# Stick-breaking attention taken head by head through eight banks, with the latents' norm moved ahead of it and the gates' sigmoid moved beside the next product

## The chip, the core and the metric

The kernel runs on one core of a Trainium2 chip. The core's engines work in parallel, each on its own stream of instructions: TensorE (PE, matmuls; PEld is its weight load), VectorE (DVE), ScalarE (ACT), GpSimd (POOL) and SyncE (SP). They wait for each other through semaphores. The metric is the device time of one execution in microseconds (us), median of several runs.

## The reference, cut to what matters

The program is a transformer layer followed by a second one, each on 256 tokens of width 2048, in fp32. The change lies in the first layer, in this part of it:

```
proj = h @ w_in                      # 2048 -> 8256 columns, split into:
c_q, c_kv (512 each), k_pe (64), q_sb, k_sb, v_sb (1024 each), gl_a, gl_b (2048 each)
# stick-breaking attention, 8 heads of 128
z = (q_sb @ k_sb.T) * 128 ** -0.5;   mask = key < query
log_beta = log_sigmoid(z)
log_one_minus = where(mask, log_sigmoid(-z), 0)
tail = reverse_cumsum(log_one_minus) - log_one_minus
a = where(mask, exp(log_beta + tail), 0);   y_b = a @ v_sb
# latents
q = rms(c_q) @ w_uq;   kv = rms(c_kv) @ w_ukv
merged = sigmoid(gl_a) * (y_a @ w_proj_mla) + sigmoid(gl_b) * (y_b @ w_proj_sb)
```

Beside all this runs `ada = silu(c) @ w_ada`, a product of one row with a matrix of 2048 x 12288.

## The kernel before

**Products with weights.** A `Gemm` takes its weights in chunks of 128 partitions x 1024 elements (512 KB). Per chunk: SP loads `raw` (four buffers, queue of SP); ACT makes the rounded half `w_hi` (L402, four buffers); DVE makes the rest `w_lo = raw - w_hi` (L431, two buffers), which also frees the `raw` buffer; PE does eight matmuls with `w_hi` (L462, the activations too are split into a high and a low half) and four with `w_lo` (L467). A full-speed chunk takes PE 2.72 us. `g_in` is `h @ w_in`; its last 64 columns are done by `Narrow` (L258 to L283). `g_psb` is the product with `w_proj_sb`, 4 units of 4 chunks; `evac_gate_b` (L1021) multiplies its result by the gate out of PSUM. `g_uq` and `g_ukv` follow. The functions in `g.beside` run between the chunks of one engine's stream.

**`ada`** is spread in slots beside other work. One slot (`ada.multiply`) is two DVE instructions (L336 at a block's start, L338 later) on one of four buffers of `w_ada`, 512 KB here, which POOL reloads when a slot has used it. Eight slots are a block, closed by one sum (L343); PE sums the block over partitions (`ada.sum`, L354) and DVE takes it (`ada.take`, L366). The table `stations` says how many slots stand at each place; the station `(None, 0, 0)` is the attention.

**The attention between `g_in` and `g_psb`.** Every engine's stream is written out by hand, in this order:

- PE transposes q and k (L586, 32 matmuls, ring `ps_turn` of three PSUM banks), DVE copies them out (L701). PE computes the masked scores of eight heads (L724 to L727) in a ring of the four banks `ps_gemm`; DVE copies each to `zs` (L754, 128 x 384).
- By halves of four heads (128 x 1536): DVE makes abs(z) (L758), ACT makes exp(-abs z) (L782) and ln(1 + that) (L786), DVE makes `mz` = max(z,0) + that (L764) and writes min(z,0) - that back to `zs` (L766). Four `ada` slots stand between L758 and L764.
- PE makes the tails of each head from `mz` (L735 to L737); DVE subtracts them from `zs` (L770); ACT takes exp (L789); PE multiplies with v (L745, L746); ACT and DVE split the result into `yt_hi` (L792) and `yt_lo` (L774).
- DVE does four more `ada` slots; ACT does the latents' squares and root (L662, L666) behind `yt_hi`; DVE inverts and scales the latents (L676, L966); PE transposes them (L498, two latents of two units each, eight matmuls a latent); ACT and DVE split them (L558, L538). The second latent's transposes wait until the first is split. Then `g_psb` starts.

ACT also does the sigmoid of both gates (L798, two instructions of 4096 elements) before the attention's own work. A change of ACT's function set costs an `ACT_TABLE_LOAD`.

Of the kernel before, what the change touches and what calls it, by code (L numbers as in the profile page):

```python
# [15 lines left out]
P = 128  # L16
# [127 lines left out]
def program(nc, A, out):  # L144
# [560 lines left out]
    z_filled, z_copied, z_abs, z_soft = sem("z_filled"), sem("z_copied"), sem("z_abs"), sem("z_soft")  # L705
    m_ready, lb_ready = sem("m_ready"), sem("lb_ready")
    tail_filled, arg_ready, a_ready = sem("tail_filled"), sem("arg_ready"), sem("a_ready")
# [253 lines left out]
    def lat_vector(dve):  # L961
# [5 lines left out]
        for turn in turn_lat:  # L967
            turn.vector(dve)
# [1685 lines left out]
```

## Time and profile before

| what | value |
| --- | --- |
| median of 3 runs | 2732.0 us (2729.41 to 2737.89) |
| the profiled execution | 2730.92 us; span from its first to its last instruction 2729.0 us |
| mean granted TensorE clock | 0.984 of full speed |
| busy share of the span | PE 95%, DVE 62%, ACT 43%, POOL 5% |
| `w_lo` (L431), mean of one | 1.22 us |
| the chain that ended last | PE 91%, DVE 5%, issue 1%, DMA 1%, ACT 1% |

The profile page divides the span in 40 slices of 68 us and gives tenths of busy time. The PE row reads 9 almost throughout, with a 6 in the slice of the attention (409 to 477 us), where DMA reads 2 and 98 GB/s. In a timeline, a row is one or several like instructions: start, time they cover, engine, line, tiles, and in brackets the idle time before the first with what ended it. A granted clock of 1.00 is 2.4 GHz and 0.50 is 1.2 GHz.

### The profile page before, as it was taken

To read this page: it belongs to the slowest core of one execution; us is meant where nothing else is said; L and a number is where in the kernel's file an instruction comes from. 1 tells how busy PE (TensorE), PEld (TensorE's weight loads), DVE (VectorE), ACT (ScalarE), POOL (GpSimd) and SP (SyncE) were. 2 spreads that over 40 slices of the span, in tenths; PEclk is the share of its full clock that TensorE was granted. 3 is DMA by queue.
4 is the path that set the end of the run, shared out by engine and by line. 5 is a ranking of instruction groups with operands and counts; after the bars stand their busy time and mean duration, and the time that the engine had idled before them with its cause. 6 is when DMAs were issued, how large, how long until landed. Compare 5 with 4: busy or idle time off the path is not lost.

```text
span 2729.0 us, 33054 instructions
## 1 busy us (share of the span) xinstructions
PE 2592.2 (95%) x12109; PEld 2142.2 (78%) x12109; DVE 1691.5 (62%) x2227; ACT 1180.0 (43%) x1506; POOL 149.2 (5%) x211
## 2 busy tenths in 40 slices
PE   3999996959989999999999999999999999999998
PEld 3878885747878888888888888878878888888886
DVE  6888987788867764545445565457654545454444
ACT  2543434334454444444334544534454444444443
POOL 1211110111101100000000000000000000000000
PEclk9999998989999999999999999999999999999999
DMA  8988892846958866666655656531366666665554
GB/s 303 332 282 273 298 313 98 293 144 223 322 159 281 278 206 192 185 192 200 192 193 190 190 162 183 179 117 47 120 189 186 191 187 190 189 188 185 194 194 158
DMA packets 269003, 559.41 MB, mean 205 GB/s; under 512 B 22784, under 2 KB 24528, under 8 KB 268240
## 3 DMA queue, kind: packets, MB, share of 16 engines
q1 hardware_dynamic: 235216, 453.57, 53.2%
q0 software_dynamic: 26752, 96.48, 10.7%
q10 hardware_dynamic: 6912, 7.73, 0.8%
q8 instruction: 76, 1.25, 0.2%
q14 instruction: 47, 0.39, 0.0%
HBM read 555.60 MB, written 2.11 MB: 204 GB/s over the span
## 4 chain that ended last, share of the span: by engine, by line
PE 91%; DVE 5%; issue 1%; DMA 1%; ACT 1%; SPq 0%; DVEq 0%; ACTq 0%
PE ps L462 55%; PE ps L467 28%; DMA ada_raw<-in_w_ada 1%; PE ps L498 1%; DVE acc L338 1%; PE ps L2311 1%; PE ps L1398 1%; PE ps L354 1%; PE ps L2167 1%; DVE acc_odd L338 1%; DVE w_lo L431 0%; PE ps L2340 0%; PE ps L276 0%; PE ps L2322 0%; ACT w_hi L402 0%
## 5 line engine op out<-in xcount | busy, mean ns | idle before, releaser
L431 DVE TENSOR_TENSOR w_lo<-raw,w_hi 128x1024 fp32r<-128x1024 f32 x846 | 1033.6, 1223 | 848.4 <-PE ps L467 773.1
L402 ACT ACTIVATE w_hi<-raw 128x1024 fp32r<-128x1024 f32 x846 | 893.5, 1062 | 1165.6 <-PE ps L467 439.7
L462 PE MATMUL ps<-w_hi,xt_hi 128*128 128x512 f32 x2496 | 987.8, 396 | 14.8 <-ACT w_hi L402 10.6
L462 PE MATMUL ps<-w_hi,xt_lo 128*128 128x512 f32 x2496 | 976.0, 391 | 0.0
L467 PE MATMUL ps<-w_lo,xt_hi 128*128 128x512 f32 x2496 | 669.3, 390 | 0.3 <-DVE w_lo L431 0.3
L462 PEld LDWEIGHTS ps<-w_hi,xt_hi 128*128 128x128 f32 x2496 | 470.8, 189 | 115.7 <-issue 11.2
L467 PEld LDWEIGHTS ps<-w_lo,xt_hi 128*128 128x128 f32 x2496 | 469.5, 188 | 100.2 <-DVE w_lo L431 1.4
L462 PEld LDWEIGHTS ps<-w_hi,xt_lo 128*128 128x128 f32 x2496 | 471.2, 189 | 94.7
L462 PE MATMUL ps<-w_hi,ht_hi 128*128 128x512 f32 x704 | 274.7, 390 | 0.0
L462 PE MATMUL ps<-w_hi,ht_lo 128*128 128x512 f32 x704 | 274.0, 389 | 0.0
L467 PE MATMUL ps<-w_lo,ht_hi 128*128 128x512 f32 x704 | 188.2, 389 | 0.0
L314 POOL DMA_DIRECT2D ada_raw<-in_w_ada x192 | 138.8, 723 | 825.8 <-DVE acc_odd L338 576.8
L467 PEld LDWEIGHTS ps<-w_lo,ht_hi 128*128 128x128 f32 x704 | 132.1, 188 | 27.5
L462 PEld LDWEIGHTS ps<-w_hi,ht_lo 128*128 128x128 f32 x704 | 132.2, 188 | 27.3
L462 PEld LDWEIGHTS ps<-w_hi,ht_hi 128*128 128x128 f32 x704 | 132.2, 188 | 27.2
L338 DVE SCALAR_TENSOR_TENSOR acc<-ada_raw,ccol,acc 128x512 f32<-128x512 f32 (+1 forms) x182 | 128.1, 704 | 10.2 <-DMA ada_raw<-in_w_ada 10.1
L338 DVE SCALAR_TENSOR_TENSOR acc_odd<-ada_raw,ccol,acc_odd 128x512 f32<-128x512 f32 (+1 forms) x182 | 128.0, 703 | 0.0
L462 PE MATMUL ps<-w_hi,yt_hi 128*128 128x512 f32 x128 | 51.8, 405 | 3.7 <-ACT w_hi L402 3.7
L462 PE MATMUL ps<-w_hi,yt_lo 128*128 128x512 f32 x128 | 50.9, 398 | 0.0
L2507 POOL DMA_DIRECT2D w1k<-in_cmp_w_k x4 | 3.0, 752 | 734.2 <-PE ps L467 734.2
L958 DVE TENSOR_TENSOR proj<-ps,proj 128x512 f32<-128x512 f32 x64 | 40.9, 681 | 2.5 <-PE ps L467 2.5
L2383 ACT ACTIVATE pb<-ps,nst 128x128 f32<-128x128 f32 x64 | 26.3, 416 | 36.8 <-DVE nst L2359 36.8
(359 smaller groups left out, 1582.4 us busy)
## 6 DMA issues: line engine op xcount, KB each, us to landing
raw<-in_w_in SPq DMA_DIRECT2D x208, 512.0 KB, 4.6
raw<-in_w_ffn_in SPq DMA_DIRECT2D x176, 512.0 KB, 3.8
ada_raw<-in_w_ada POOLq DMA_DIRECT2D x128, 512.0 KB, 5.6
raw<-in_w_ffn_out SPq DMA_DIRECT2D x88, 512.0 KB, 4.6
raw<-in_w_gate SPq DMA_DIRECT2D x88, 512.0 KB, 3.7
raw<-in_w_up SPq DMA_DIRECT2D x88, 512.0 KB, 4.4
raw<-in_w_down SPq DMA_DIRECT2D x88, 512.0 KB, 4.3
raw<-in_w_out SPq DMA_DIRECT2D x64, 512.0 KB, 4.4
```

Source lines behind the costliest of these rows:

```text
L314: sp.dma_start(self.tile(v), wview("w_ada")[:, ADA_K * s:ADA_K * (s + 1), col:col + width]).then_inc((ada_first if v < 2 * self.per else a ...
L338: ins = dve.scalar_tensor_tensor(part, rows[:, k, :], weight, part, ALU.mult, ALU.add)
L354: mm = pe.matmul(ps_ada[:, at_i:at_i + 1], acc[:, b % 2, i * P:(i + 1) * P], ones[:, 0:1], start=True, stop=True)
L402: act.activation(w_hi[:, w % HI, :, :], raw[:, w % RAW, :, :], ACT.Copy).then_inc(hi_ready, 1)
L431: dve.tensor_tensor(w_lo[:, w % LO, :, :], raw[:, w % RAW, :, :], w_hi[:, w % HI, :, :].bitcast(F32), ALU.subtract).then_inc(raw_used, 1)
L462: pe.matmul(bank[t][:, :], g.lhs(part, g.k0 + 2 * s + k, t), w_hi[:, w % HI, k, :], start=(s == 0 and k == 0 and part == 0), stop=False)
L467: mm = pe.matmul(bank[t][:, :], g.lhs(0, g.k0 + 2 * s + k, t), w_lo[:, w % LO, k, :], start=False, stop=(s == g.S - 1 and k == 1))
L498: mm = pe.transpose(ps_turn[n % 3][:, k * SEQ + t * P:k * SEQ + (t + 1) * P], self.src(2 * v + k, t), ident)
L958: last = nc.vector.tensor_tensor(p, ps_gemm[2 * (c % 2) + t][:, :], p, ALU.add)
L1398: mm = pe.transpose(ps_turn[v][:, k * SEQ + t * P:k * SEQ + (t + 1) * P], hbuf[:, t, (2 * v + k) * P:(2 * v + k + 1) * P], ident)
L2167: mm = pe.matmul(ps_ada[0:60, 0:256], fl[i][:, u, :, :].rearrange("p h i -> p (h i)"), w1[i][:, u, :], start=(u == 0), stop=(u == 15))
L2311: pe.matmul(bank[:, lo:up], qrT[:, 4 * a + m, t * P:(t + 1) * P], ksw[br][:, a, b, 0:(t + 1) * P], start=True, stop=False)
```

## The change

1. **By head.** abs, exp and ln are done per head, in place in `mz` (named `soft(h)`); abs moves from DVE to ACT. The write-back of min(z,0) - ln(...) is gone: PE's matrices become minus (strictly after or equal) and minus ones (`neg_upto`, `neg_ones`, made by two DVE instructions), so that z plus the bank is the argument of exp. Scores, and then tails, have one bank per head out of all eight; the products with v use banks 0 to 3.
2. **`ada`.** Six slots instead of eight stand in the attention: three behind the scores, one each behind the arguments of heads 0, 2 and 4. The other two stand in units 0 and 1 of `g_psb`, which then have one beside every chunk. The take of the last block of `g_in` stands before the attention.
3. **Latents.** Squares and root stand on ACT ahead of `Narrow`'s copy; inverse and scaling stand on DVE ahead of the attention. The transposes stay behind it.
4. **Gates.** The sigmoid is four ACT instructions of 2048 elements, one behind each of the first four `w_hi` of `g_psb`.

```diff
 def sb_tensor(pe):
+        pe.wait_ge(ada_taken, ada.sums)
         for h in range(H):
-            pe.wait_ge(turn_scaled, turn_sb.at + 2 * (h // 2) + 2)
-            if h - 3 > 0:
-                pe.wait_ge(z_copied, h - 3)
-            b = ps_gemm[h % 4]
+            pe.wait_ge(turn_scaled, turn_sb.at + (2 * (h // 2) + 2 if h < 5 else 8))
+            b = ps[h]
...
         for h in range(H):
-            pe.wait_ge(m_ready, h // 4 + 1)
-            pe.matmul(b[:, 0:SEQ], after, mz[h // 4][:, h % 4, 0:SEQ], start=True, stop=False)
+            pe.wait_ge(m_ready, h + 1)
+            pe.matmul(b[:, 0:SEQ], neg_upto[:, :], soft(h)[:, 0:SEQ], start=True, stop=False)
...
 def sb_vector(dve):
-        ada.multiply(dve, 4)
+        ada.multiply(dve, 3)
         for h in range(H):
+            dve.wait_ge(z_log, h + 1)
+            dve.scalar_tensor_tensor(soft(h), zs[:, h, :], 0.0, soft(h), ALU.max, ALU.add).then_inc(m_ready, 1)
+        for h in range(H):
             dve.wait_ge(tail_filled, h + 1)
-            dve.tensor_tensor(zs[:, h, :], zs[:, h, :], ps_gemm[h % 4][:, 0:BL], ALU.subtract).then_inc(arg_ready, 1)
+            dve.tensor_tensor(zs[:, h, :], zs[:, h, :], ps[h][:, 0:BL], ALU.add).then_inc(arg_ready, 1)
+            if h in SB_SLOTS:
+                ada.multiply(dve, SB_SLOTS[h])
...
+    def gates_piece(act, i):
+        if i == 0:
+            act.wait_ge(evac_done, g_in2.c + 1)
+        c0, c1 = ((GB0, NIN), (GA0, GB0))[i // 2]
+        act.activation(proj[:, i % 2, c0:c1], proj[:, i % 2, c0:c1], ACT.Sigmoid).then_inc(gates_ready, 1)
+    SB_SLOTS = {0: 1, 2: 1, 4: 1}
...
-    stations += [(None, 0, 0, 8)]
-    stations += [(g_psb, u, s, 1 if s < 3 else 0) for u in range(4) for s in range(4)]
+    stations += [(None, 0, 0, 6)]
+    stations += [(g_psb, u, s, 1 if s < 3 or u < 2 else 0) for u in range(4) for s in range(4)]
...
 def _(act):
+            rms_lat.scalar(act)
             g_in2.copied(act)
             g_in2.scalar(act, lambda t: proj[:, t, 8192:NIN])
-            gates_scalar(act)
             sb_scalar(act)
-            rms_lat.scalar(act)
...
 def _(dve):
+            lat_vector(dve)
+            ada.take(dve, len(ada_takes[None, 0, 0]))
             sb_vector(dve)
-            ada.multiply(dve, 4)
-            lat_vector(dve)
-            dve.wait_ge(gates_ready, 2)
+            lat_turns_vector(dve)
```

ACT's stream from `Narrow`'s copies to the attention's last exp, before (`ez` is the buffer of four heads each):

```order
L263 ACTIVATE proj<-ps 128x64 x2
L798 ACT_TABLE_LOAD
L798 ACTIVATE proj<-proj 128x4096 x2
L782 ACT_TABLE_LOAD
L782 ACTIVATE ez<-ez 128x1536 x2
L786 ACT_TABLE_LOAD
L786 ACTIVATE ez<-ez,const 128x1536 x2
L789 ACT_TABLE_LOAD
L789 ACTIVATE zs<-zs 128x384 x8
```

The same place now, for the first two of the eight heads and then the end:

```order
L263 ACTIVATE proj<-ps 128x64 x2
L775 ACTIVATE mz_99<-zs 128x384
L777 ACT_TABLE_LOAD
L777 ACTIVATE mz_99<-mz_99 128x384
L775 ACTIVATE mz_99<-zs 128x384
L777 ACTIVATE mz_99<-mz_99 128x384
...
L780 ACT_TABLE_LOAD
L780 ACTIVATE mz_99<-mz_99,const 128x384 x4
L780 ACTIVATE mz_100<-mz_100,const 128x384 x4
L783 ACT_TABLE_LOAD
L783 ACTIVATE zs<-zs 128x384 x8
```

The two long sigmoids are gone from here; abs (L775) and exp (L777) alternate with a single table load, and ln (L780) follows for all heads.

DVE's stream from the last `yt_lo` to the first `w_lo` of `g_psb`, before (`acc`, `acc_odd` are slots of `ada`):

```order
L774 TENSOR_TENSOR yt_lo<-ps,yt_hi 128x512 x4
L338 SCALAR_TENSOR_TENSOR acc<-ada_raw,ccol,acc 128x512
L338 SCALAR_TENSOR_TENSOR acc_odd<-ada_raw,ccol,acc_odd 128x512
...
L343 TENSOR_TENSOR acc<-acc,acc_odd 128x512
L676 RECIPROCAL stat<-stat 128x4
L966 TENSOR_SCALAR proj<-proj,stat 128x512 x4
L538 SCALAR_TENSOR_TENSOR lat_lo<-ps,cols,lat_hi 128x256 x8
L431 TENSOR_TENSOR w_lo<-raw,w_hi 128x1024
```

And now:

```order
L767 TENSOR_TENSOR yt_lo<-ps,yt_hi 128x512 x4
L538 SCALAR_TENSOR_TENSOR lat_lo<-ps,cols,lat_hi 128x256 x8
L431 TENSOR_TENSOR w_lo<-raw,w_hi 128x1024
```

The four slots, the block's sum, the inverse and the scaling no longer stand between `yt_lo` and the latents' split.

ACT's stream at the start of `g_psb` now (before, the `w_hi` rows follow each other):

```order
L558 ACTIVATE lat_hi<-ps,cols 128x256 x8
L402 ACTIVATE w_hi<-raw 128x1024
L793 ACT_TABLE_LOAD
L793 ACTIVATE proj<-proj 128x2048
L402 ACTIVATE w_hi<-raw 128x1024
L793 ACTIVATE proj<-proj 128x2048
```

Each of the first four conversions is followed by a piece of the sigmoid.

## Rows read from the trace of the kernel before

**Rows 1.** Two stretches, all engines; busy us, count, granted clock, DMA share, GB/s.

```profile
434.64:445.06 10.42, 0.00 (x0) 0.00 (x0) 10.35 (x13) 7.89 (x6) 2.89 (x4) 0.64 0.36 108
...
461.88:469.76 7.88, 0.00 (x1) 0.01 (x1) 7.75 (x15) 3.30 (x8) 2.89 (x4) 0.68 0.58 174
```

**Rows 2.** DVE in order of time: start us, us, line, out<-in, [idle before <-releaser].

```profile
428.68 0.54 DVE L754 COPY zs<-ps 128x384 f32<-128x384 f32 x1
...
434.68 0.56 DVE L754 COPY zs<-ps 128x384 f32<-128x384 f32 x1 [0.32 <-PE ps L727]
...
435.15 3.42 DVE L758 SCALAR_TENSOR_TENSOR ez<-zs 128x1536 f32<-128x1536 f32 x2
...
439.28 0.74 DVE L338 SCALAR_TENSOR_TENSOR acc<-ada_raw,ccol,acc 128x512 f32<-128x512 f32 x1
...
443.25 1.75 DVE L764 SCALAR_TENSOR_TENSOR mz<-zs,ez 128x1536 f32<-128x1536 f32 x1
...
468.03 1.67 DVE L966 TENSOR_SCALAR proj<-proj,stat 128x512 f32<-128x512 f32 x4
```

**Rows 3.** ACT in order of time, same columns.

```profile
421.61 0.38 ACT L258 ACTIVATE w_in_rest_turned<-ps 64x256 f32<-64x256 f32 x1 [12.80 <-PE ps L276]
...
424.06 7.13 ACT L798 ACTIVATE proj<-proj 128x4096 f32<-128x4096 f32 x2
...
440.11 1.28 ACT L786 ACT_TABLE_LOAD   x1
...
441.40 3.04 ACT L786 ACTIVATE ez<-ez,const 128x1536 f32<-128x1536 f32 x2
...
444.46 1.28 ACT L789 ACT_TABLE_LOAD   x1
...
450.76 1.45 ACT L789 ACTIVATE zs<-zs 128x384 f32<-128x384 f32 x3 [5.02 <-DVE zs L770]
```

**Rows 4.** PE in order of time, same columns.

```profile
423.22 4.47 PE L586 MATMUL ps<-const,proj 128*128 128x128 f32 x32
...
445.06 1.22 PE L735 MATMUL ps<-mz,const 128*128 128x256 f32 x2 [10.42 <-DVE mz L764]
...
455.12 0.60 PE L745 MATMUL ps<-zs,proj 128*128 128x256 f32 x2
...
460.14 0.38 PE L746 MATMUL ps<-zs,proj 128*128 128x128 f32 x2
...
469.76 1.97 PE L498 MATMUL ps<-const,proj 128*128 128x128 f32 x8 [9.23 <-DVE proj L966]
...
473.57 1.97 PE L498 MATMUL ps<-const,proj 128*128 128x128 f32 x8 [1.84 <-DVE lat_lo L538]
```

**Rows 5.** The chain of waits: start us, us, what.

```profile
474.72 0.84 ACT lat_hi L558 x2
...
476.41 0.95 ACT w_hi L402
...
477.50 3.75 PE ps L462 x8
...
481.25 1.25 PE ps L467 x4
...
486.18 1.81 PE ps L462 x8
```

**Rows 6.** Two stretches of 2 us in which the granted clock falls.

```profile
436.00:438.00 2.00, 0.00 (x0) 0.00 (x0) 2.00 (x2) 1.07 (x1) 0.00 (x0) 0.87 0.00 0
...
464.00:466.00 2.00, 0.00 (x0) 0.00 (x0) 2.00 (x4) 1.20 (x2) 0.95 (x2) 0.69 0.52 100
```

**Rows 7.** ACT's conversion of chunk 7 of the product with w_proj_sb.

```profile
492.98 1.06 ACT L402 ACTIVATE w_hi<-raw 128x1024 fp32r<-128x1024 f32 x1 [2.66 <-DMA raw<-in_w_proj_sb]
```

**Rows 8.** The chain at the same chunk.

```profile
499.93 1.81 PE ps L462 x8
```

**Rows 9.** Ten us with one w_ada slot beside every chunk.

```profile
170.00:180.00 10.00, 10.00 (x49) 8.38 (x48) 8.97 (x14) 3.86 (x4) 2.60 (x4) 1.00 0.97 330
```

More of the change, by code:

```diff
@@ L704, in program @@
                      for d, c, s in ((qsb, Q0, sb_scale), (ksb, K0, 1.0))])
-    z_filled, z_copied, z_abs, z_soft = sem("z_filled"), sem("z_copied"), sem("z_abs"), sem("z_soft")
-    m_ready, lb_ready = sem("m_ready"), sem("lb_ready")
-    tail_filled, arg_ready, a_ready = sem("tail_filled"), sem("arg_ready"), sem("a_ready")
+    z_filled, z_copied, z_abs, z_exp, z_log = (sem(f"z_{n}") for n in ("filled", "copied", "abs", "exp", "log"))
+    m_ready, neg_ready, arg_ready = sem("m_ready"), sem("neg_ready"), sem("arg_ready")
+    tail_filled, a_ready = sem("tail_filled"), sem("a_ready")
     yb_filled, yb_hi, yb_lo = sem("yb_filled"), sem("yb_hi"), sem("yb_lo")
@@ L778, in sb_scalar @@
     def sb_scalar(act):
-        for f in range(2):
-            ef = ez[:, 4 * f:4 * f + 4, :].rearrange("p a b -> p (a b)")
-            act.wait_ge(z_abs, f + 1)
-            act.activation(ef, ef, ACT.Exp, scale=-1.0).then_inc(z_abs2, 1)
-        for f in range(2):
-            ef = ez[:, 4 * f:4 * f + 4, :].rearrange("p a b -> p (a b)")
-            act.wait_ge(z_abs2, f + 1)
-            act.activation(ef, ef, ACT.Ln, bias=ones[:, 0:1]).then_inc(z_soft, 1)
+        act.wait_ge(turn_scaled, turn_sb.end)
+        for h in range(H):
+            act.wait_ge(z_copied, h + 1)
+            act.activation(soft(h), zs[:, h, :], ACT.Abs).then_inc(z_abs, 1)
+            act.wait_ge(z_abs, h + 1)
+            act.activation(soft(h), soft(h), ACT.Exp, scale=-1.0).then_inc(z_exp, 1)
+        for h in range(H):
+            act.wait_ge(z_exp, h + 1)
+            act.activation(soft(h), soft(h), ACT.Ln, bias=ones[:, 0:1]).then_inc(z_log, 1)
         for h in range(H):
@@ L1018, in evac_gate_b @@
         col = Count(GB0 + CW * u, 2 * CW, j).value
+        if u == 0 and j is None:
+            nc.vector.wait_ge(gates_ready, 4)
         for t in range(T):
@@ L1480, in program @@
             ada_sums.setdefault(later[1] if g else later[0], []).append(done)
-            ada_takes.setdefault(later[2] if g else later[1], []).append(done)
+            taken = later[1] if g and later[1][0] is None else later[2] if g else later[1]
+            ada_takes.setdefault(taken, []).append(done)
             done += 1
```

56 lines of the change are left out of this document (20 added, 36 removed).

## The prediction

> **What bounds the kernel now.** I read the page first: PE is busy 95% of the span and carries 91% of the chain, so time can only be won where PE waits. The slices show one such place inside the change's reach, the attention at 421 to 477 us. I then took the windows of that place, the timelines of DVE, ACT and PE, and the chain. Three things are to be seen.
>
> First, between scores and tails PE does nothing for 10.42 us while DVE works 10.35 of them [rows 1]. DVE copies the last score from 434.68, spends 3.42 us on abs, then four slots of w_ada (a slot is two instructions of 0.74 us that overlap a little, 1.33), and begins `mz` at 443.25 [rows 2]; the first tail starts at 445.06 [rows 4]. Second, the tails run 445.06 to 455.12 and the products with v until 460.52 (460.14 + 0.38), back to back. Third, PE is idle again for 9.23 us, until the latents are scaled [rows 4]: DVE is busy 7.75 of 7.88 us with slots, inverse and scaling [rows 1]. The latents' two rounds follow, 469.76 and 473.57 [rows 4], then `g_psb` at 477.50 [rows 5]. So the stretch is a chain of DVE and ACT work, hardly PE's.
>
> **The change part by part.**
>
> *The beginning.* The latents' squares and root go into ACT's idle 12.80 us before 421.61 [rows 3]; about 4 us of work is covered entirely. Inverse and scaling (1.67 us, [rows 2]) fall where DVE waits for the first transposes, so they are free too. New ahead of DVE's first copy are a take and the two instructions that make the matrices. They follow PE's sum, which ends when the transposes begin at 423.22 [rows 4]; the first unit of transposes takes 4.47 / 8 = 0.56 us, which covers most of them. I charge +0.15 us; the nearest rows bound it between 0 and one more 0.74 us instruction.
>
> *Scores to first tail.* DVE's copies start 0.86 us apart ((434.68 - 428.68) / 7) [rows 2]. ACT's chain starts when the first is out, 428.68 + 0.54 + 0.15 = 429.4. Abs and exp of 384 elements have the shape of the exps in [rows 3]: three in 1.45 us, so 0.52 for one and 0.465 for each overlapped. Abs, table load 1.28, exp: 429.4 + 0.55 + 1.28 + 0.52 = 431.8. Seven more pairs, each waiting on its own abs (0.52 + 0.04 + 0.47 = 1.03): 439.0. Load 1.28: 440.3. The two ln of 1536 take 3.04 together [rows 3]; for 384 I estimate 0.6 for one and 0.51 apart. First ln out at 440.9, last at 444.4. DVE has done its three slots by 439 (435.4 + about 3.5), so it is ACT that ends last here. One `mz` of 384 is like the copy, 0.56 us: the first tail starts at 441.5 against 445.06, **-3.55 us**. The bounds are zero gain (ACT's many small instructions eat it) and -6 us (ACT as fast as DVE's copies come).
>
> The ln and exp loads here stand in the chain, where before they stood beside DVE's work. The row of the load shows 1.28 us and the next ACT instruction begins at 441.40, 0.01 us after its end [rows 3]. The Trainium skill (ScalarE: Activation LUTs, What ACT_TABLE_LOAD costs) adds a drain of 1.38 us to each load's 1.283, 2.66 in all; by that the two loads ahead of the first tail would cost 2.8 us more and the time would be 2720.3. The trace disagrees with the drain, so I leave it out.
>
> *Tails and products.* As before, PE has idled over 5 us by 441.5. The clock fell 2.9 us after the first stop (0.87 over 436 to 438 puts the fall at 437.5) and 4.2 us after the second (0.69 over 464 to 466 puts it at 464.8) [rows 6]. So the tails begin at the lower level, 1.2 GHz, as they did, and take the same 10.06 us: 451.6. DVE must keep up: the arguments start behind the last `mz`, 445.0, and take 8 x 0.5 + 3 slots x 1.33 = 8.0 us, so the last is out at about 453 and its exp at 453.5. The product of the last head is due at 451.6 + 7 x 0.675 = 456.3, so PE remains the bound, with 2.8 us to spare. Products end at 451.6 + 5.40 = 457.0. Moving slots in between the arguments costs nothing while that spare lasts.
>
> *Products to latents.* The wait of 9.24 us (460.52 to 469.76) goes: scaled latents are ready, their banks free. **-9.24 us.** What is late next is ACT, which must do the last `yt_hi` before the first `lat_hi`: 0.69 us behind the products' end, where the cold transposes took 469.76 to 470.91, 1.15 us (the first split of the second round starts at 474.72, 1.15 behind 473.57) [rows 4, 5]. That is -0.46. The second round's transposes take 0.6 at 2.4 GHz instead of 1.15, -0.55. The ends from the same rows are 0 and -1.0 for both together, **-1.0 us**. From the second split to PE's start everything is as before (474.72 to 477.50, 2.78). Sum: 477.50 - 3.55 - 9.24 - 1.0 = 463.7, a gain of 13.8.
>
> *The first chunks of g_psb.* Chunk 0 took 3.75 + 1.25 = 5.0 us at 1.2 GHz where a full-speed chunk takes 1.81 + 0.91 = 2.72 [rows 5]. Two things now meet. PE's pauses before it become two of about 2.3 us instead of one of 9.2 and two of 1.8, and both observed falls needed 2.9 and 4.2 us of idleness, so the clock may stay up. But ACT now puts a load and 1.85 us of sigmoid behind each conversion (7.13 / 4 = 1.8 plus start-up) [rows 3]: conversion 1 is out 4.2 us after conversion 0, later ones 2.85 apart. With the high clock PE then waits 1.4 us for chunk 1 and 0.13 for each of the next two, and reaches chunk 4 at 4 x 2.72 + 1.4 + 0.26 = 12.5 us from its start, against 5.0 + 3 x 2.72 = 13.2 at the low clock (a sum over partitions of some 0.8 us comes on top of either). With the low clock ACT is hidden and nothing changes. I take the middle, **-0.4 us**.
>
> [...]
>
> *The two slots moved into g_psb.* On DVE a chunk with a slot costs 1.22 (the page's mean for `w_lo`) + 1.33 = 2.55 us against PE's 2.72, and `w_lo` may be 3 us late before PE notices; hidden. On DMA, units 0 and 1 ask for 1.049 MB per 2.72 us, 385 GB/s. The stretch with one smaller slot (512 + 384 KB a chunk, 337 GB/s asked) ran at 330 GB/s with PE busy 10.00 of 10 us [rows 9]. At 330 the extra 1.05 MB put the loads 3.2 us behind. ACT's conversion of chunk 7 ends at 494.04 and PE takes it at 499.93: 5.9 us of cover [rows 7, 8]. So 0, and 3.2 us if that cover is gone; the value taken is 0.
>
> **Sum.** -3.55 - 9.24 - 1.0 - 0.4 = -14.2 (the +0.15 is inside the first term). The span goes from 2729.0 to 2714.8; with the 1.9 us outside it the profiled execution, 2730.92, becomes 2716.7. The median before, 2732.0, stands 1.1 above its profiled execution; the forecast is 2732.0 - 14.2, rounded to 2717.5 us.
>
> **The rivals.**
>
> *Cover lost in g_psb.* Conversions behind four sigmoids, and loads at 385 GB/s, make PE wait. For it: ACT's cadence, 2.85, is above PE's 2.72, and ACT waits for DMA at chunk 7 already (2.66 us) [rows 7]. Against it: 5.9 us of cover. Price 2 us (sigmoids with a high clock) to 6 us (3.2 more from DMA): 2720 to 2724, centre 2721.5.
>
> *The attention itself gains nothing.* ACT has 24 small instructions, 16 of them in a dependent chain; if each dependent pair costs 0.5 us more than estimated, the first tail starts at 445 again and only the latents' part remains: 2732.0 - 10.6 = 2721.4. For it: ACT is what ends last there. Against it: waits between engines in these timelines cost some 0.04 us.
>
> *The clock stays up.* If it does not fall before 441.5, the tails save up to 3.0 us (eight heads at 0.88 instead of 10.06), and chunk 0 its 0.4: 2714. Against it: the falls at 2.9 and 4.2 us of idleness.
>
> *Slower.* `g_psb` starved by its loads. Units 0 and 1 need 8.4 MB; at a rate R they take 8.4 / R instead of 21.8 us. Above 230 GB/s the loss, with the cover counted, stays below the gain; at 200 GB/s it is 42 - 21.8 - 5.9 = 14.3 us and the time 2732; at 170 GB/s it is 21.7 us and the time 2739. It decides from about 200 GB/s down. Against it: 330 GB/s over ten us with the same two queues [rows 9].
>
> **How the numbers follow.** Forecast 66%, own range 2714 to 2720.5; cover lost 17%; no gain in the attention 8%; clock up 6%; slower 3%. About 0.3%, 8.2 us, is what a measurement of this kernel can tell from no change: the line lies at 2723.8. All of the forecast and the clock case, and most of the next two, lie below it: faster 0.89. Same 0.08 is the upper end of the two middle cases, slower 0.03. The range 2712.5 to 2723.5 takes in both ends of the forecast and nearly all of the middle cases.
>
> **What would show it.** Right: the first tail at 441 to 442 with ACT's ln before it; one 10 us run of tails; the latents' transposes at once behind the products; `g_psb` at 463 to 464.5; PE gapless in `g_psb` but for at most 2 us before chunk 1; the rest of the trace shifted by 14 us. Wrong: table loads between abs and exp; a wait of an argument or an exp that PE feels; PE waiting for `w_hi` with a DMA behind it in chunks 5 to 10; or a later stage that takes the gain back.

## The result, and the profile after

| | before | after |
| --- | --- | --- |
| median | 2733.68 us (2729.41 to 2737.89, 4 runs) | 2718.28 us (2714.57 to 2720.21, 4 runs) |
| the profiled execution | 2730.92 us, span 2729.0 us | 2719.46 us, span 2716.9 us |

The ratio is 0.9942, with an interval of 0.9922 to 0.9962: 15.4 us off the median. The two profiled executions show only 12.1 of them in their spans: the one before is 2.8 us faster than its median, the one after, the slowest but one of its four, 1.2 us slower.

PE in order of time in the kernel after, same columns as [rows 4]. Line numbers moved by a few; L742 and L743 are now the products with v.

```profile
440.14 1.19 PE L735 MATMUL ps<-mz,neg_upto 128*128 128x256 f32 x2 [6.49 <-DVE mz L759]
...
448.70 0.60 PE L742 MATMUL ps<-zs,proj 128*128 128x256 f32 x2
...
453.73 0.38 PE L743 MATMUL ps<-zs,proj 128*128 128x128 f32 x2
453.95 1.04 PE L498 MATMUL ps<-const,proj 128*128 128x128 f32 x8
457.22 1.09 PE L498 MATMUL ps<-const,proj 128*128 128x128 f32 x8 [2.24 <-DVE lat_lo L538]
460.57 0.77 PE L462 MATMUL ps<-w_hi,yt_hi 128*128 128x512 f32 x1 [2.26 <-DVE lat_lo L538]
...
464.83 0.39 PE L462 MATMUL ps<-w_hi,yt_hi 128*128 128x512 f32 x1
```

The tails start 19.51 us behind `Narrow`'s copy (420.63 below; 445.06 - 421.61 = 23.45 before), the latents' transposes stand right behind the last product, and where PE waited 9.23 us there is nothing. What is left are two short pauses of 2.24 and 2.26 us. ACT, answering to [rows 3]:

```profile
420.63 0.38 ACT L258 ACTIVATE w_in_rest_turned<-ps 64x256 f32<-64x256 f32 x1 [11.10 <-PE ps L276]
...
428.34 0.52 ACT L775 ACTIVATE mz<-zs 128x384 f32<-128x384 f32 x1 [6.57 <-DVE zs L754]
...
437.49 1.28 ACT L780 ACT_TABLE_LOAD   x1
438.79 4.16 ACT L780 ACTIVATE mz<-mz,const 128x384 f32<-128x384 f32 x8
442.96 1.28 ACT L783 ACT_TABLE_LOAD   x1
...
454.15 0.60 ACT L786 ACTIVATE yt_hi<-ps 128x512 fp32r<-128x512 f32 x1 [0.71 <-PE ps L743]
454.64 1.56 ACT L558 ACTIVATE lat_hi<-ps,cols 128x256 fp32r<-128x256 f32 x4
...
459.35 1.07 ACT L402 ACTIVATE w_hi<-raw 128x1024 fp32r<-128x1024 f32 x1
...
463.55 1.05 ACT L402 ACTIVATE w_hi<-raw 128x1024 fp32r<-128x1024 f32 x1
```

and DVE, answering to [rows 2]:

```profile
433.69 0.56 DVE L754 COPY zs<-ps 128x384 f32<-128x384 f32 x1 [0.32 <-PE ps L730]
...
439.43 4.10 DVE L759 SCALAR_TENSOR_TENSOR mz<-zs,mz 128x384 f32<-128x384 f32 x8 [1.75 <-ACT mz L780]
...
449.75 1.47 DVE L762 TENSOR_TENSOR zs<-zs,ps 128x384 f32<-128x384 f32 x3
...
455.51 1.66 DVE L538 SCALAR_TENSOR_TENSOR lat_lo<-ps,cols,lat_hi 128x256 fp32r<-128x256 f32 x4
...
460.46 1.23 DVE L431 TENSOR_TENSOR w_lo<-raw,w_hi 128x1024 fp32r<-128x1024 f32 x1
```

DVE has done its three slots by 437.7 and waits for ACT's first ln [1.75 <-ACT mz L780]: ACT sets the first tail. Two windows, columns as [rows 1], the wait for the tails and ten us inside `g_psb` with a slot beside every chunk:

```profile
433.66:440.14 6.48, 0.00 (x1) 0.03 (x1) 4.70 (x9) 6.33 (x12) 2.17 (x3) 0.71 0.47 134
480.00:490.00 10.00, 10.00 (x45) 8.26 (x44) 9.96 (x15) 4.25 (x4) 2.68 (x4) 1.00 1.01 373
```

In the second PE is busy 10.00 of 10 us while the DMA engines are full and move 373 GB/s.

By pieces, from the copy (421.61, 420.63) on:

| piece | before | after | change | forecast |
| --- | --- | --- | --- | --- |
| copy to first tail | 23.45 | 19.51 | -3.94 | -3.55 |
| tails (first tail to first product) | 10.06 | 8.56 | -1.50 | 0 |
| products with v | 5.40 | 5.41 | 0 | 0 |
| wait for the latents | 9.24 | -0.16 | -9.40 | -9.24 |
| the latents' two rounds | 7.74 | 6.62 | -1.12 | -1.0 |
| sum | 55.89 | 39.94 | -15.95 | -13.8 |
| `g_psb`, chunk 0 to chunk 4 (PE) | 13.96 | 13.27 | -0.69 | -0.4 |

Counted from the copy, the changed kernel is 16 us ahead at `g_psb` and 16.5 at `g_ukv`. From there to `g_pmla`, the product behind MLA attention, it loses 7 us in this execution, in stages that the change doesn't touch: 1.6 in `g_ukv` and 5.3 in MLA attention. PE at the same place of MLA attention in the profiled execution (L1135 are its scores):

```profile
578.04 3.67 PE L586 MATMUL ps<-const,proj 128*128 128x128 f32 x16 [24.58 <-DVE pe_out L1093]
...
590.07 0.74 PE L1135 MATMUL ps<-kT,proj 128*128 128x128 f32 x2
...
591.55 1.17 PE L1135 MATMUL ps<-kT,proj 128*128 128x256 f32 x2
```

and in another execution of the same kernel (experiment `e1_again`):

```profile
589.75 0.44 PE L1135 MATMUL ps<-kT,proj 128*128 128x128 f32 x2
...
590.60 0.65 PE L1135 MATMUL ps<-kT,proj 128*128 128x256 f32 x2
```

The scores take 0.74 and 1.17 us in the one and 0.44 and 0.65 in the other. The windows say why:

```profile
590.00:595.00 5.00, 5.00 (x16) 3.02 (x15) 2.95 (x9) 0.93 (x5) 0.72 (x1) 0.50 0.15 23
```
```profile
590.00:595.00 5.00, 5.00 (x27) 3.03 (x25) 4.87 (x14) 1.83 (x8) 0.72 (x1) 1.00 0.22 48
```

A granted clock of 0.50 against 1.00: the clock, back at 583 after a pause of 24.6 us, fell a second time at 590, 2 us after a pause of 1.14 us had ended (587.88) and with PE working, in one execution and not in the other. `g_ukv` shows the same on a smaller scale. Behind a pause of 1.4 us its first chunk starts at the high clock in both, and in the one execution the clock falls within it:

```profile
530.00:532.00 2.00, 2.00 (x6) 1.54 (x5) 1.85 (x3) 0.11 (x1) 0.35 (x1) 0.52 0.90 295
```
```profile
532.00:534.00 2.00, 2.00 (x10) 1.65 (x10) 2.00 (x4) 0.00 (x0) 0.26 (x1) 1.00 0.84 256
```

The first row is the profiled execution, the second `e1_again` at the same place.

### The profile page after: what moved, and what is told of

It reads as the page before. It is cut to its first block, busy times and chain, and to the rows that moved or that the text cites. A ratio compares the mean times of both kernels' runs of the same rounds, so it can differ in the third digit from the quotient of the medians.

```text
span 2716.9 us, 33069 instructions
## 1 busy us (share of the span) xinstructions
PE 2592.0 (95%) x12109; PEld 2140.9 (79%) x12109; DVE 1684.6 (62%) x2231; ACT 1183.6 (44%) x1527; POOL 149.2 (5%) x211
## 4 chain that ended last, share of the span: by engine, by line
PE 91%; DVE 4%; DMA 2%; ACT 1%; issue 1%; SPq 0%; DVEq 0%; ACTq 0%
PE ps L462 55%; PE ps L467 28%; DMA ada_raw<-in_w_ada 1%; PE ps L1398 1%; PE ps L498 1%; PE ps L354 1%; PE ps L2314 1%; PE ps L2170 1%; DVE acc L338 1%; PE ps L2343 0%; DVE w_lo L431 0%; PE ps L276 0%; DMA raw<-in_w_out 0%; PE ps L1137 0%; DVE acc_odd L338 0%
## 5 line engine op out<-in xcount | busy, mean ns | idle before, releaser
L462 PE MATMUL ps<-w_hi,xt_hi 128*128 128x512 f32 x2496 | 987.0, 395 | 15.1 <-ACT w_hi L402 10.8
```

The lines of the kernel that those rows point to most:

```text
L462: pe.matmul(bank[t][:, :], g.lhs(part, g.k0 + 2 * s + k, t), w_hi[:, w % HI, k, :], start=(s == 0 and k == 0 and part == 0), stop=False)
```

## The experiments

Every kernel was timed beside the kernel before on its own chip. In the tables "stretch" runs from `Narrow`'s copy on ACT to the first `w_lo` of `g_psb`, "tails" is the part of it from the first tail to the first product with v, and "MLA" runs from the first `w_lo` of `g_ukv` to the first of `g_pmla`; all are differences of starts in the profiled execution. All profiled executions, in us:

| kernel | copy at | stretch | tails in it | to `g_ukv` | MLA | rest | span |
| --- | --- | --- | --- | --- | --- | --- | --- |
| before | 421.6 | 55.8 | 10.1 | 67.3 | 87.9 | 2096.3 | 2729.0 |
| after | 420.6 | 39.8 | 8.6 | 66.9 | 94.9 | 2094.7 | 2716.9 |
| e1_again | 420.1 | 41.2 | 10.0 | 67.5 | 88.0 | 2094.9 | 2711.7 |
| e12_again | 421.6 | 39.9 | 8.7 | 66.9 | 94.9 | 2094.9 | 2718.2 |
| e2_norm_alone | 421.8 | 51.2 | 9.4 | 67.3 | 87.9 | 2094.8 | 2723.0 |
| e3_norm_slots | 421.3 | 50.4 | 10.8 | 66.7 | 94.9 | 2094.9 | 2728.1 |
| e4_head_alone | 419.9 | 52.8 | 9.1 | 66.9 | 95.0 | 2097.8 | 2732.4 |
| e5_gates_back | 423.5 | 42.5 | 8.7 | 68.2 | 93.2 | 2097.9 | 2725.4 |
| e6_preload | 418.7 | 39.6 | 9.0 | 66.8 | 94.9 | 2094.7 | 2714.6 |
| e7_lat_ring | 421.8 | 38.3 | 8.6 | 67.0 | 94.7 | 2096.9 | 2718.7 |
| e8_warm | 421.8 | 39.6 | 7.1 | 66.8 | 94.8 | 2094.6 | 2717.7 |
| e9_all | 421.6 | 37.4 | 9.3 | 67.0 | 89.4 | 2098.2 | 2713.6 |
| e10_mla_warm | 424.6 | 41.3 | 10.0 | 67.5 | 95.7 | 2094.6 | 2723.7 |
| e11_all_mla | 420.0 | 37.1 | 8.8 | 67.0 | 87.3 | 2096.2 | 2707.6 |

Copy, stretch, "to `g_ukv`", MLA and rest add up to the span. A stretch repeats within 1.5 us (39.8, 39.9, 41.2, and 41.3 in `e10_mla_warm`, whose edit lies behind it), and all of that is in the tails: without them the four are 31.26 or 31.27 us, and the kernel before is 45.77. The MLA column jumps by 7. It has two parts that come separately: `g_ukv` takes 1.6 us more in seven of the 14 profiles, MLA attention 5.3 to 7.7 more in nine of them, `e3_norm_slots` with the old phases among these. Copy and rest move by up to 5.9 and 3.6 us without any edit there. So a single span or a median of six says less of an edit than its stretch does.

**e1_again and e12_again: the changed kernel unaltered.**

> The changed kernel once more, unaltered. The stretch from ACT's first copy behind the narrow product to PE's first matmul with w_proj_sb took 55.9 us before and 39.9 us after; nearly all of this should repeat. In the changed kernel's profile TensorE's clock fell a second time inside the later attention (590 to 604 us), and that stage took 5.3 us longer than before. Theory: this second fall belongs to how the pauses happen to lie in one execution, so it may be missing here, and the time ratio stays at 0.994 plus or minus 0.0015. Rival: the change shifts that stage so that the fall comes every time; then it is there again and the low stretch is again about 13 us.

> The changed kernel unaltered, beside the three others: the time 2714 to 2719 us. Its profile falls in one of two groups: MLA attention 87.9 us and a span of 2711 to 2713, or 94.9 us and 2716 to 2719. By the theory the two differ in TensorE's low clock 10 to 20 us into the stage's matmuls and in nothing else.

Measured: 2715.24 us (2712.43 to 2720.29, 6 runs), ratio 0.9940 [0.9921, 0.9959], and on the other chip 2720.17 us (2715.48 to 2725.39, 6 runs), ratio 0.9950 [0.9931, 0.9969]. One profile is without the second fall (MLA 88.0, span 2711.7), one has it (94.9, 2718.2). What the profile of the change seemed to lose in MLA attention (the 5.3 us of the expectation, 7 with `g_ukv`) is no part of the change: one kernel shows both. `e12`'s median lies 1.2 us above what its expectation allowed.

The three stretches of the changed kernel differ in one thing, how soon the granted clock is back at 1.00 after the first tail: 3.0 us in the first profile, 3.2 in e12, 5.9 in e1 (and 6.2 in the kernel before). The tails take 8.6, 8.7 and 10.0 us accordingly. The first four chunks of `g_psb`, which also start at the low clock, go the same way: 13.27, 13.34 and 13.95 us on PE, where the kernel before takes 13.96.

**e2_norm_alone: the kernel before with squares, root, inverse and scaling ahead of the attention.**

```diff
+        pe.wait_ge(yb_lo, 4)
         for turn in turn_lat:
...
+            rms_lat.scalar(act)
             g_in2.copied(act)
...
-            rms_lat.scalar(act)
...
+            lat_vector(dve)
             sb_vector(dve)
             ada.multiply(dve, 4)
-            lat_vector(dve)
+            lat_turns_vector(dve)
```

> The kernel before, with only the latents' squares, root, inverse and scaling moved ahead of the attention (the four w_ada slots still stand on DVE between yt_lo and the latents' split; PE waits for yt_lo ahead of the latents' transposes, which their banks need). Theory: of the 9.2 us of idle PE only the norm's 1.9 us and the transposes' start go, because DVE's slots (6.0 us) stand in the same queue: the stretch is 52 us (gain 3 to 4.5 us). Rival, that the norm is the whole wait: 46.5 us.

Measured: 2727.6 us (2723.43 to 2733.71, 10 runs), ratio 0.9980 [0.9966, 0.9995]; stretch 51.2, 4.7 less than before, 0.6 of which is the clock in the tails (9.4 for 10.1). DVE and PE behind the attention:

```profile
461.32 0.74 DVE L338 SCALAR_TENSOR_TENSOR acc<-ada_raw,ccol,acc 128x512 f32<-128x512 f32 x1
...
467.34 1.65 DVE L538 SCALAR_TENSOR_TENSOR lat_lo<-ps,cols,lat_hi 128x256 fp32r<-128x256 f32 x4
```
```profile
461.50 1.07 PE L498 MATMUL ps<-const,proj 128*128 128x128 f32 x8 [1.46 <-issue]
469.05 1.97 PE L498 MATMUL ps<-const,proj 128*128 128x128 f32 x8 [6.48 <-DVE lat_lo L538]
```

PE transposes the first latent 1.46 us behind the products (461.50; this edit has it wait for the last `yt_lo`) and then waits 6.48 us: DVE's split of that latent stands behind four slots and the block's sum. The wait of 9.24 us has moved by one round, and 7.9 of it are still there.

**e3_norm_slots: the same, and the four slots one each behind the arguments of heads 0, 2, 4 and 6.**

```diff
                               ALU.subtract).then_inc(arg_ready, 1)
+            if h % 2 == 0:
+                ada.multiply(dve, 1)
...
-            ada.multiply(dve, 4)
```

> As the run with the norm alone, and the four slots behind yt_lo are put behind the arguments of heads 0, 2, 4 and 6. Heads are not taken singly and the gates' sigmoid stays ahead. Theory: the wait between products and latents is gone, the rest is unchanged: the stretch is 46.5 to 47.5 us (8.5 to 9.4 us less than before), at most 0.5 us lost where the last argument comes late. Rival, that taking the heads singly carries the gain: under 3 us.

Measured: 2731.17 us (2726.03 to 2734.81, 10 runs), ratio 0.9987 [0.9971, 1.0002]; stretch 50.4. The time can't be told from the kernel before. Theory and rival both missed the stretch: 5.4 us less, not 8 to 9, nor under 3. Where it went, DVE, ACT and PE at the end of the products:

```profile
459.09 0.55 DVE L770 TENSOR_TENSOR zs<-zs,ps 128x384 f32<-128x384 f32 x1
```
```profile
460.10 1.55 ACT L794 ACTIVATE yt_hi<-ps 128x512 fp32r<-128x512 f32 x3
```
```profile
461.55 0.67 PE L745 MATMUL ps<-zs,proj 128*128 128x256 f32 x2 [1.96 <-DVE yt_lo L776]
```

By phases the arguments start only when DVE has written `zs` back, and four slots behind them put the last argument at 459.09. The last exp waits for it, `yt_hi` of the first heads is queued behind that exp on ACT, `yt_lo` behind `yt_hi`, and PE's products wait 1.96 us for a bank that `yt_lo` frees. PE's last product ends 2.9 us later than before (41.85 against 38.92 behind the copy), 2.2 of it in the products and 0.7 in the tails, most of which are waits for a bank of the old ring of four. That takes back 2.9 of the 7.8 us of waiting behind the products that went (9.24 before, 1.46 now).

**e4_head_alone: by head in eight banks, and norm, slots and sigmoids where they were.**

```diff
-            rms_lat.scalar(act)
             g_in2.copied(act)
             g_in2.scalar(act, lambda t: proj[:, t, 8192:NIN])
+            for i in range(4):
+                gates_piece(act, i)
             sb_scalar(act)
+            rms_lat.scalar(act)
...
-        ada.multiply(dve, 3)
+        ada.multiply(dve, 4)
...
-    SB_SLOTS = {0: 1, 2: 1, 4: 1}
+    SB_SLOTS = {}
...
-            lat_vector(dve)
             ada.take(dve, len(ada_takes[None, 0, 0]))
             sb_vector(dve)
+            ada.multiply(dve, 4)
+            lat_vector(dve)
             lat_turns_vector(dve)
```

> The changed kernel with only its attention by head kept: norm, sigmoid and w_ada slots stand as before (eight slots, four of them behind yt_lo, sigmoid ahead of the attention). Theory: ACT's sigmoid delays the first abs by 1.9 us, so the first tail comes 2 us earlier than before instead of 3.9; the 9.2 us behind the products are back. The stretch is 52.5 to 54 us. Rival, that heads carry the gain: 44 to 46 us.

Measured: 2735.83 us (2730.9 to 2741.87, 10 runs), ratio 1.0008 [0.9993, 1.0023]; stretch 52.8.

```profile
441.32 1.19 PE L735 MATMUL ps<-mz,neg_upto 128*128 128x256 f32 x2 [8.44 <-DVE mz L759]
...
465.01 1.97 PE L498 MATMUL ps<-const,proj 128*128 128x128 f32 x8 [9.24 <-DVE proj L962]
```

The first tail comes 21.46 us behind the copy, 2.0 earlier than before and 2.0 later than in the changed kernel; then the old wait, 9.24 us for DVE's scaling. By head alone gives 3 us of stretch, 2.0 by the first tail and 1.0 because the clock came back sooner in the tails (9.1 us for 10.1), and no time that these runs can tell.

So norm and slots gain 5.4 us of stretch, by head 3.0, the gates 1.3 to 2.7 (next experiment), together 9.7 to 11.1, and the whole change 14.6 to 16.0. Some 4 to 6 us come only from the parts' meeting. Without the tails, in which the clock differs from one execution to the next, the whole is 14.5. By head, DVE has room for slots between the arguments: the first argument starts 3.3 us behind the first tail (443.45, 440.14), in the old phases 5.1 (450.18, 445.06). But the changed kernel also has two slots and the block's sum less there than e3, and no run moves these two alone, so how the 4 to 6 us divide between room and less work isn't shown.

**e5_gates_back: the changed kernel with the four sigmoid pieces ahead of the attention.**

```diff
+            for i in range(4):
+                gates_piece(act, i)
             sb_scalar(act)
...
-        if u == 0:
-            gates_piece(eng, s)
```

> The changed kernel with the four pieces of the gates' sigmoid ahead of the attention's ACT work again. Theory: the load and the pieces take 8.6 us from 421.8 on ACT, 1.9 us past the point where the first abs could begin, and ACT is the bound between scores and tails: the first tail 1.9 us later, the stretch 41.8 us; the first four chunks of the product with w_proj_sb get back 0.9 us of waits, so about 1 us is lost in all. Rival: it was covered before and still is, no change in the stretch, and 0.9 us gained.

Measured: 2724.17 us (2721.19 to 2729.24, 10 runs), ratio 0.9963 [0.9951, 0.9976]; stretch 42.5, 1.3 to 2.7 more than the changed kernel.

```profile
425.99 7.31 ACT L793 ACTIVATE proj<-proj 128x2048 f32<-128x2048 f32 x4
433.20 0.51 ACT L775 ACTIVATE mz<-zs 128x384 f32<-128x384 f32 x1
```

The first abs waits for the sigmoids (433.20 is 9.67 us behind the copy; in the changed kernel 428.34 - 420.63 = 7.71), and the first tail comes at 21.46 instead of 19.51. That is the 2 us by which by head alone fell short. The 0.9 us that the first chunks were expected to give back did not come: chunk 0 to chunk 4 took 14.64 us on PE, with chunk 0 at the low clock throughout (13.27 and 13.95 in the changed kernel). The median is 4.6 us above the next kernel's beside it. The first tail explains 2 of them; the rest stays unexplained, as the two profiled spans differ by 10.8 us, 4.9 of them ahead of the edit and 3.2 in the column of the rest.

**e6_preload: a one-column exp ahead of the first abs, so that the table load leaves the chain.**

```diff
+            act.wait_ge(eps_set, 1)
+            act.activation(stat[:, 31:32], epsc[:, 0:1], ACT.Exp)
             sb_scalar(act)
```

> The changed kernel with one exp of a single column on ACT ahead of the first abs, so that the exp table is loaded while ACT waits. Theory: ACT's chain is the bound between scores and first tail, so the stretch shortens by the load, 1.3 us (39.9 to 38.6). Rival: DVE or the scores are the bound: no change.

Measured: 2719.60 us (2716.39 to 2722.93, 4 runs), ratio 0.9955 [0.9938, 0.9971]; stretch 39.6.

```profile
436.88 1.19 PE L735 MATMUL ps<-mz,neg_upto 128*128 128x256 f32 x2 [5.20 <-DVE mz L759]
```

The first tail comes 18.23 us behind the copy, 1.28 earlier: just the load. But the clock now falls before the latents' second round instead of behind it (that round takes 1.97 us instead of 1.09), the two rounds take 0.56 us more and the tails 0.45, and 0.3 us are left of 1.3.

**e7_lat_ring: the second latent's transposes wait for their own bank only.**

```diff
-            if max(n - 2, self.at) > 0:
-                pe.wait_ge(turn_scaled, max(n - 2, self.at))
+            first = self.at if self.ring is None else self.ring
+            if max(n - 2, first) > 0:
+                pe.wait_ge(turn_scaled, max(n - 2, first))
```

> The changed kernel with the second latent's transposes waiting for two units back in their ring and not for the whole first latent. Theory: the two rounds behind the products (6.6 us) are bound by that wait; ACT and DVE run through, 1.6 us less (39.9 to 38.3), and the clock of the first chunk may change. Rival: ACT's eight splits in a row bound it: under 0.5 us.

Measured: 2718.73 us (2717.08 to 2720.82, 4 runs), ratio 0.9946 [0.9929, 0.9962]; stretch 38.3, as expected.

```profile
455.15 1.48 PE L500 MATMUL ps<-const,proj 128*128 128x128 f32 x12
457.64 0.66 PE L500 MATMUL ps<-const,proj 128*128 128x128 f32 x4 [1.01 <-DVE lat_lo L540]
```

Twelve matmuls go in one run and the pause is 1.01 us instead of 2.24. In the time it is lost among executions. Chunk 0 of `g_psb` now starts at the high clock (0.47 and 0.40 us a matmul) and falls to the low one with its fifth matmul (0.45, then 0.63).

**e8_warm: 88 small matmuls that nothing reads, in PE's wait for the tails.**

```diff
+        pe.wait_ge(z_copied, H)
+        for _ in range(88):
+            pe.matmul(ps[7][:, 0:P], ident16[:, :], maskz, start=True, stop=True)
         pe.wait_ge(neg_ready, 2)
```

> The changed kernel with 88 small bf16 matmuls (masked constants into a bank that is overwritten later) while PE would idle between scores and tails. Theory: the low clock at the tails goes, 8 x 0.875 = 7.0 us instead of 8.56, the stretch 1.5 us shorter; and the clock stays high until the first chunk of the product with w_proj_sb only if its own pauses don't drop it. Rival: DVE's arguments and ACT's exps follow the tails at 1.0 us a head and eat the gain: under 0.5 us.

Measured: 2716.52 us (2715.29 to 2719.5, 4 runs), ratio 0.9938 [0.9921, 0.9955]; stretch 39.6, 0.2 to 1.6 less than the changed kernel.

```profile
435.50 5.09 PE L733 MATMUL ps<-masks,ident 128*128 128x128 bf16 x88 [0.65 <-DVE zs L757]
441.33 0.67 PE L738 MATMUL ps<-mz,neg_upto 128*128 128x256 f32 x2 [0.75 <-DVE mz L762]
...
452.11 0.70 PE L745 MATMUL ps<-zs,proj 128*128 128x256 f32 x2 [0.24 <-ACT zs L786]
...
457.60 1.97 PE L498 MATMUL ps<-const,proj 128*128 128x128 f32 x8 [2.39 <-DVE lat_lo L538]
```

The clock stays up: the first tail's matmuls take 0.67 us instead of 1.19. But PE now reaches a product before its exp (0.24), the products take 5.9 us instead of 5.4 and end 1.0 us earlier than in the first profile of the changed kernel (2.4 earlier than in e1's), and the second round of the latents is at the low clock (1.97). By the end of the products the tails' low clock costs 1.0 to 2.4 us, as the clock's return falls, since DVE and ACT come next.

**e9_all: the edits of e6 and e7 together, abs of heads 5 to 7 on DVE, and one slot moved from behind the scores to behind the argument of head 6.** The diff shows the last two.

```diff
+            if h > 4:
+                dve.wait_ge(z_copied, h + 1)
+                dve.scalar_tensor_tensor(soft(h), zs[:, h, :], -1.0, zs[:, h, :], ALU.mult, ALU.max).then_inc(z_abs, 1)
-        ada.multiply(dve, 3)
+        ada.multiply(dve, 2)
...
-    SB_SLOTS = {0: 1, 2: 1, 4: 1}
+    SB_SLOTS = {0: 1, 2: 1, 4: 1, 6: 1}
```

> The changed kernel with four edits at once: the exp functions are loaded before the first abs; the abs of heads 5 to 7 is on VectorE; the second latent's transposes wait only for their bank; two slots of w_ada behind the scores and one each behind the arguments of heads 0, 2, 4 and 6. Theory (ScalarE's chain sets the first tail, the latents' ring costs 1.5 us): the first tail starts 17.0 to 17.5 us behind Narrow's copy, where the changed kernel has 19.5; g_psb starts 1.5 us earlier again from the ring; the stretch from that copy to g_psb's first w_lo is 36 to 37.5 us (39.8 and 41.2 in the two profiles of the changed kernel) and the time 2 to 4 us below the changed kernel's. Rival (TensorE's clock gives back whatever the first tail gains, as with the early load alone, where 1.3 us less idleness made the stretch only 0.3 shorter): 38 to 39.5 us and the same time within 1.5 us.

Measured: 2717.0 us (2712.47 to 2721.94, 6 runs), ratio 0.9942 [0.9922, 0.9962]; first tail at 17.81 (0.3 above the expectation), stretch 37.4, median 3.2 below the changed kernel's beside it, which the two intervals (0.9922 to 0.9962 and 0.9931 to 0.9969) can't tell apart. The rival, a clock that gives everything back, is refuted for the stretch.

```profile
459.02 0.47 PE L462 MATMUL ps<-w_hi,yt_hi 128*128 128x512 f32 x1 [1.97 <-ACT w_hi L402]
...
463.10 0.50 PE L462 MATMUL ps<-w_hi,yt_hi 128*128 128x512 f32 x1 [1.08 <-ACT w_hi L402]
```

Here chunk 0 of `g_psb` runs at the high clock (0.47 and 0.40 a matmul instead of 0.77 and 0.63), and PE waits 1.08 us for chunk 1's conversion, behind the sigmoid. Chunk 0 to chunk 4 is 13.26 us on PE, against 13.27, 13.34 and 13.95 in the changed kernel: warm with the wait costs what cold with an early return of the clock does.

**e10_mla_warm: the changed kernel with 380 small matmuls in PE's pause ahead of MLA attention.**

```diff
+        for _ in range(380):
+            pe.matmul(ps[7][:, 0:P], ident16[:, :], maskq, start=True, stop=True)
         pe.wait_ge(hn, 14)
         turn_qk.tensor(pe)
```

> The changed kernel with 380 small matmuls whose result nothing reads, in TensorE's 24.6 us without work ahead of MLA attention's transposes (22 us of work at the high clock). Theory (the 7 us by which most profiles' MLA attention is longer, 94.9 against 87.9 us, are a second fall of TensorE's clock, and it needs the low clock of the first): no low stretch from the end of g_ukv on, the first 16 transposes in 2.3 instead of 3.7 us, the stage (first w_lo of g_ukv to first w_lo of g_pmla) 85.5 to 86.5 us, the median 3 to 8 us below that of the changed kernel. Rival (the second fall comes from the thin work of the stage itself): the stage stays at 92 to 95 us and the time within 2 us of the changed kernel's. Second rival (the stage is bound by VectorE): 87.9 us without any low clock.

Measured: 2714.22 us (2711.74 to 2727.71, 9 runs), ratio 0.9943 [0.9924, 0.9961]. The nine lie in two groups, five at 2711.7 to 2714.2 (mean granted clock 0.992 to 0.994) and four at 2721.0 to 2727.7 (0.985 or 0.986). The profile is one of the upper group, and its MLA stage 95.7 us. The groups lie some 12 us apart, more than the 5.3 to 7.7 of the second fall, and what else divides them is open.

```profile
557.75 21.39 PE L1126 MATMUL ps<-masks,ident 128*128 128x128 bf16 x380
582.49 3.05 PE L586 MATMUL ps<-const,proj 128*128 128x128 f32 x16 [3.35 <-DVE pe_out L1093]
```
```profile
565.00:570.00 5.00, 5.00 (x94) 5.00 (x92) 4.58 (x5) 1.60 (x2) 0.00 (x0) 1.00 0.01 3
...
580.00:585.00 5.00, 2.51 (x15) 2.51 (x16) 4.08 (x6) 0.00 (x0) 0.00 (x0) 0.82 0.00 0
585.00:590.00 5.00, 5.00 (x33) 4.06 (x32) 4.79 (x8) 0.00 (x0) 0.00 (x0) 0.84 0.00 0
590.00:595.00 5.00, 3.87 (x17) 2.29 (x17) 2.27 (x7) 0.00 (x0) 0.00 (x0) 0.84 0.01 3
595.00:600.00 5.00, 5.00 (x15) 2.76 (x14) 3.26 (x10) 1.83 (x8) 0.72 (x1) 0.50 0.34 98
```

The long low stretch of the pause is gone (1.00 where it was 0.50), and the second fall comes all the same, before 595 (0.84, then 0.50). So my theory that it needs that long stretch is refuted. But the matmuls end 3.35 us before the transposes, and from 583.2, 0.7 us into the transposes, the clock is low for some 3.4 us (0.82 over 580 to 585 and 0.84 over 585 to 590), so that the first 16 take 3.05 us instead of 3.67 and not the 2.3 expected. Whether the second fall needs any low clock ahead of it is therefore not shown; e11, which has the same short stretch and no second fall, says only that this isn't enough. The rival, that it comes from the stage's own thin work, isn't refuted and isn't shown.

**e11_all_mla: both.**

> The four edits of the third kernel back and the 380 small matmuls together. If both work and do not meet: the stretch 36 to 37.5 us, the MLA stage 86 us, the time 2707 to 2711 us, 5 to 11 below the changed kernel's. If only the matmuls work, 2710 to 2713; if only the four edits, 2713 to 2716; if neither, 2716 to 2719.

Measured: 2712.07 us (2707.51 to 2720.17, 6 runs), ratio 0.9926 [0.9906, 0.9946]; stretch 37.1, MLA 87.3, span 2707.6. It beats the kernel before by 20 us and, by medians beside each other, the changed kernel by 8.1; of that second difference the two intervals (0.9926 and 0.9950) overlap, so its size is uncertain. A stage without the second fall takes 87.3 us here, 0.7 less than with the pause's low clock, not the 2 I expected: the short low stretch in the transposes is there too, and behind them PE waits for DVE (1.14 us for the copy of the last ones). By the granted clock (0.992 and more) five of the six executions belong to the lower group of e10.

## Why the prediction was right

The forecast was 2717.5 us, and the median is 2718.28; the gain forecast was 14.5 and 15.4 came. (The sum itself gives 14.2 and 2717.8; it was set down as 2717.5.) That the two times differ by only 0.8 us is luck: three medians of the same changed kernel are 2715.24, 2718.28 and 2720.17, gains of 19.2, 15.4 and 12.0 us. What the working got right is the stretch, -14.5 us outside the tails against -13.8, and how a single execution then comes out depends on the clock: in the profiled one the tails gave 1.5 us more, and 7 went again in `g_ukv` and MLA attention.

*Scores to first tail, -3.55.* Right in size and in cause: -3.94. The +0.15 for the take and the matrices was nothing: the first score's copy starts 7.07 us behind `Narrow`'s copy in both kernels. ACT ends last, DVE waits 1.75 us for it. A pair of abs and exp starts every 0.97 us instead of 1.03, which is the 0.4. The ln load ends at 437.49 + 1.28 = 438.77 and the first ln starts at 438.79. The drain that the Trainium skill (ScalarE: Activation LUTs, What ACT_TABLE_LOAD costs) adds is not there either: its 2.8 us for two loads would, by an estimate, have put the first tail at 22.3. That moving the sigmoid away is 2 of the 4 us (e4, e5) was not in my working: I took ACT's chain to start when the first score is out, which is so only without the sigmoids.

*Tails, 0.* Mis-sized: -1.5 and -1.4 in two profiles with these instructions unaltered, -0.1 in the two others (e1, e10). The clock does fall before 441.5, as said, but it came back 3.0 us after the first tail instead of the 6.2 us in the execution of [rows 4]. I had taken the return from a single execution of the kernel before for a constant, and e2, with the same tails at the same place, takes 9.4 us and not 10.06.

*The wait of 9.24.* Right, and the term on which all hung. The experiments add what the sum hid: it is no property of the norm's move. With the norm alone it goes and 6.48 us come back a round later (e2); with the slots between the arguments of the old phases 2.9 us come back by the end of the products (e3). "Costs nothing while that spare lasts" was true of the new order only. The spare of 2.8 us was 1.5 (the last exp ends at 451.78, its product starts at 453.29), since the tails were quicker.

*Latents' rounds, -1.0.* -1.12.

*First chunks of `g_psb`, -0.4.* -0.69 in this profile, 0 in e1: chunk 0 starts at the low clock in every profile of the changed kernel. It took 4.26 us here (460.57 to 464.83), between the 5.0 of [rows 5] and the 2.72 of a warm one, because the clock came back within it, and 4.94 in e1. The forecast was the middle of two cases, clock up and clock down; what came was clock down, for which the working had no gain, and the gain came from the clock's earlier return. The cadence behind the sigmoids was 4.20 us (459.35 to 463.55) as worked out, and the wait of PE with the high clock, forecast as 1.4 us, was 1.08 where it occurred (e9). Chunk 0 starts at the low clock in the changed kernel, after pauses of 2.24 and 2.26 us, and at the high one in e9, after pauses of 1.02 and 1.97.

*The two slots, 0.* Right: no wait of PE in `g_psb`, at 373 GB/s.

*The rivals.* Cover lost: no row of it. Attention gains nothing: refuted by 19.51. Clock stays up: e8 made it so, and by the end of the products it is worth 1.0 us against one profile of the changed kernel and 2.4 against another, not 3, since exps come next. `g_psb` starved: the DMA engines gave more than the 330 GB/s of [rows 9].

*The signs.* The first tail was to come at 441 to 442 and came at 440.14, 441.1 when the earlier copy (by 0.98) is taken out. `g_psb` was to start at 463 to 464.5 and starts at 461.6 on the same count, 2.1 us ahead of the sum's 463.7: 1.5 of it are the tails, the rest the 0.4, 0.2 and 0.1 of the other terms.

*A later stage that takes the gain back* stood among the things that would make the prediction wrong. The profile shows one, 7 us in `g_ukv` and MLA attention, and only a second profile of the same kernel could show that it is no effect of the change. How often it comes in either kernel, and what decides it, stays open. That it comes about equally often in both isn't shown either: the medians, which differ by about what the stretch gives, only fit that.

## What to carry to other kernels

Before a wait is booked as gained, ask which instruction of the waited engine stands next in the queue: moving one piece of work shows the next (6.48 us here), and parts that gained 10 to 11 us of stretch one by one gained some 15 together. Work is free between two instructions only if the order there leaves that engine waiting; the old phases had no such place, the new order had. When a later stage that no edit touched moves by several us in a profile, profile the same kernel again before explaining it.

## What was new about the hardware

- TensorE's clock after a pause returns at different times in executions of one kernel: 3.0 to 5.9 us after the first tail, 1.4 us of stretch. All else in the stretch repeats within 0.02 us.
- It can be low while PE is busy 5.00 of 5 us by the records: 0.50 over 590 to 595 in one execution, 1.00 in another, 5.3 us of the stage, and it fell 2 us behind a pause of 1.14 us. Filling 21.4 us of the pause ahead of the stage, all but its last 3.35, doesn't prevent it (e10).
- Two pauses of only 2.24 and 2.26 us with 1.09 us of transposes between them were enough to have the low clock in what follows (0.77 and 0.63 us a matmul from 460.57). After 1.0 and 1.97 us the clock was still high (0.47 and 0.40), and stayed so in e9 but fell four matmuls later in e7 and e11.
- `ACT_TABLE_LOAD` is 1.28 us and nothing else, with 0.02 us ahead of it (the last exp ends at 437.47, the load starts at 437.49) and 0.02 behind; taking one out of the chain brought the next engine 1.28 us forward (e6).
- Two queues together gave 373 GB/s with PE at 10.00 of 10 us.
